# A hybrid decoder step on one core: natural keys in a tile of their own, late bias stores on a second semaphore, the first norm on five columns, and two conv units that share one wait

## What is computed

```python
n = rms_norm(x, g_mix);  q, k, v, hc, bc, cc = split(n @ w_in)
q, k = rms_norm(q, q_norm), rms_norm(k, k_norm)          # per head
attn = dilated_attention(q, k, v, rel_bias)              # dilations 1, 4, 16; the bias depends on the distance
conv = bc * short_conv(cc * hc, state_conv, conv_w)      # three taps
h = x + concat[rms_norm(attn, g_attn_out), rms_norm(conv, g_conv_out)] @ w_out
h = h + (silu(rms_norm(h, g_ffn) @ w_gate) * (rms_norm(h, g_ffn) @ w_up)) @ w_down
y = h + sigmoid(rms_norm(h, g_ple) @ w_ple_gate) * (p @ w_ple_proj)
```

## Time and profile before

| what | value |
|---|---|
| median of 3 runs | 2585.83 us (2585.45 to 2592.28) |
| profiled execution | 2585.61 us, of it span 2584.1 us, so 1.5 us around it |
| mean granted PE clock | 0.989 |
| PE busy | 2516.5 us (97%) |
| DVE, ACT, POOL busy | 1751.8 (68%), 950.2 (37%), 286.9 us (11%) |

### The profile page before, as it was taken

One profiled execution on the slowest core, in us unless ns is written; L12 is line 12 of the kernel. 1 busy time (PEld: TensorE's weight loads), 2 busy tenths in 40 slices (PEclk: granted clock), 3 DMA queues, 4 the chain that ended last, 5 costly groups with the idle time before them and its releaser, 6 DMA issues.

```text
span 2584.1 us, 52528 instructions
## 1 busy us (share of the span) xinstructions
PE 2516.5 (97%) x20677; PEld 2497.8 (97%) x20677; DVE 1751.8 (68%) x2181; ACT 950.2 (37%) x1283; POOL 286.9 (11%) x335
## 2 busy tenths in 40 slices
PE   8898999999989989999999999999999999999998
PEld 7898999999989979999999999999999999999998
DVE  3566777777686879889888898888433322466332
ACT  5333333343342444444444444444322211233221
POOL 2111111111021000000000000000000000142101
PEclk9999999999999989999999999999999999999999
DMA  6544333434344344445444454444665543233331
GB/s 194 159 114 126 107 112 103 122 106 113 99 127 132 118 115 115 134 130 145 130 114 133 129 144 130 114 134 130 209 207 173 159 141 116 80 89 101 107 109 58
DMA packets 482496, 328.31 MB, mean 127 GB/s; under 512 B 19382, under 2 KB 458714, under 8 KB 481400
## 3 DMA queue, kind: packets, MB, share of 16 engines
q1 hardware_dynamic: 451936, 250.74, 34.6%
q0 software_dynamic: 28848, 75.06, 9.0%
q10 hardware_dynamic: 1648, 1.65, 0.2%
HBM read 286.80 MB, written 44.91 MB: 128 GB/s over the span
## 4 chain that ended last, share of the span: by engine, by line
PE 88%; DMA 4%; DVE 4%; ACT 2%; issue 2%; POOL 0%; SPq 0%; ACTq 0%; DVEq 0%; POOLq 0%
PE acc L552 16%; PE acc L556 16%; PE acc L554 16%; PE acc L779 11%; PE acc L778 11%; PE acc L780 11%; DMA wraw<-in_w_in 2%; DMA wraw<-in_w_down 1%; ACT whi L924 1%; PE aux L594 1%; DVE wlo L1297 1%; PE aux L562 1%; DMA x_nat<-in_x_prompt 1%; PE aux L638 1%; PE aux L567 0%
## 5 line engine op out<-in xcount | busy, mean ns | idle before, releaser
L1297 DVE TENSOR_TENSOR wlo<-wraw,whi 128x1024 fp32r<-128x1024 f32 (+1 forms) x276 | 332.5, 1205 | 424.9 <-ACT whi L924 424.2
L924 ACT ACTIVATE whi<-wraw 128x1024 fp32r<-128x1024 f32 (+1 forms) x276 | 285.2, 1034 | 704.9 <-PE acc L556 593.4
L778 PE MATMUL acc<-xb_hi,whi 128*128 128x260 f32 x1232 | 349.2, 283 | 12.4 <-DVE xb_lo L1655 12.4
L779 PE MATMUL acc<-xb_lo,whi 128*128 128x260 f32 x1232 | 349.5, 284 | 0.0
L780 PE MATMUL acc<-xb_hi,wlo 128*128 128x260 f32 x1232 | 348.9, 283 | 0.0
L780 PE MATMUL acc<-xa_hi,wlo 128*128 128x260 f32 x1232 | 348.7, 283 | 0.0
L779 PE MATMUL acc<-xa_lo,whi 128*128 128x260 f32 x1232 | 348.5, 283 | 0.0
L778 PE MATMUL acc<-xa_hi,whi 128*128 128x260 f32 x1232 | 348.4, 283 | 0.0
L552 PE MATMUL acc<-slots_a,whi 128*128 128x260 f32 x1536 | 315.0, 287 | 0.0
L556 PE MATMUL acc<-slots_a,wlo 128*128 128x260 f32 x1536 | 310.2, 283 | 0.0
L554 PE MATMUL acc<-slots_a,whi 128*128 128x260 f32 x1536 | 308.4, 282 | 0.0
(11 more groups left out here) (308 smaller groups left out, 5099.7 us busy)
## 6 DMA issues: line engine op xcount, KB each, us to landing
wraw<-in_w_in SPq DMA_DIRECT2D x96, 512.0 KB, 4.0
blocks<-in_w_gate SPq DMA_DIRECT2D x88, 512.0 KB, 6.3
blocks<-in_w_up SPq DMA_DIRECT2D x88, 512.0 KB, 6.2
wraw<-in_w_down SPq DMA_DIRECT2D x48, 448.0 KB, 3.8
wraw<-in_w_out SPq DMA_DIRECT2D x32, 512.0 KB, 3.9
wraw<-in_w_ple_gate SPq DMA_DIRECT2D x32, 512.0 KB, 4.0
slots_b<-f_dram SPq DMA_DIRECT2D x28, 520.0 KB, 4.8
f_dram<-sig_t POOLq DMA_DIRECT2D x22, 520.0 KB, 3.3
```

The source lines that it names most:

```text
L778: mm(to, w_h, hi[:, n, X_OF[u], :], start=p == 0, stop=False)
L779: mm(to, w_h, lo[:, n, X_OF[u], :], start=False, stop=False)
L924: on(whi[:, u % HILO, 0:width], wraw[:, u % RAW, 0:width], ACT.Copy).then_inc(s_whi, 1)
L1297: V.tensor_tensor(wlo[:, u % HILO, 0:width], wraw[:, u % RAW, 0:width], whi[:, u % HILO, 0:width].bitcast(F32), ALU.subtract).then_inc(s_w ...
```

## The change

It has four parts. **Keys:** the natural keys get a place of their own, row 15 of `hid` (row 1 of `prob` in the last pair); their copy waits for the transposes alone, the next copy of values for the split of the values instead. In the last pair DVE's work is put in another order. **Bias stores:** S4 to S7 count on a semaphore of their own, the `load_skew` behind S7 waits for S0 to S3 alone, POOL waits for the others ahead of its loop, and S1 to S3 go out after units 8, 9 and 10. **First norm:** ACT takes the roots of the five columns ahead of its loop, DVE their reciprocals, PE then spreads the results, and DVE copies them out. **Conv half:** the first two units do seven tiles each, then the eighth; the norm's sum yields five columns, which are rooted, inverted and spread like the first; the attention of the last pair starts one unit later.

```diff
-    k_nat = v_nat
+    k_nat, k_nat_last = hid[:, KT - 1, 0:SEQ], prob[:, 1, :]
# ACT, heads, g == 9 (values) and g == 11 (keys)
+                    act.wait_ge(s_v2, j)
                 on(v_nat[:, :, :], ..., ACT.Copy).then_inc(s_natsb, 1)
...
-                    act.wait_ge(d_k, 16 * j)
-                act.wait_ge(d_v, 16 * j + 16)
-                act.wait_ge(s_v2, j + 1)
-                on(k_nat[:, :, :], ..., ACT.Copy).then_inc(s_natsb, 1)
+                on(k_nat_last if last else k_nat, aux[:, BANK_T, :], ACT.Copy).then_inc(s_natsb, 1)
# POOL
-                pool.wait_ge(d_skew, 16 * KA)
+                pool.wait_ge(d_skew, 16 * 4)
             load_skew(a + 1)
...
-            pool.wait_ge(s_unit, 6 + 2 * n)
+            pool.wait_ge(s_unit, 7 + n)
             store_skew(2 * n, 2 * n + 2)
# first norm: PE, ACT, DVE
-                    pe.wait_ge(s_xsq, QB + 1)
+                    pe.wait_ge(s_ninv, N_X)
                     for b in range(QB):
                         nc.tensor.transpose(aux[:, BANK_S, ...], gsq[:, b:b + 1].broadcast_to([P, P]), ident[:, :])
...
+        on(gsq[:, 0:QB], gsq[:, 0:QB], ACT.Sqrt, bias=EPS, scale=1.0 / D_MODEL)
+        on(gsq[0:DEC, QB:QB + 1], ..., ACT.Sqrt, ...).then_inc(s_nroot, 1)
         pair(FIRST, 0, None)
...
+            if a is None and g == 3:
+                dve.wait_ge(s_nroot, N_X)
+                V.reciprocal(gsq[:, 0:QB], gsq[:, 0:QB])
+                V.reciprocal(gsq[0:DEC, QB:QB + 1], ...).then_inc(s_ninv, 1)
+            if a is None and g == 4:
+                dve.wait_ge(s_nsum, N_X)
+                V.tensor_copy(rstd[:, 0:SEQ], aux[:, BANK_S, :])
+                V.tensor_copy(rstd[:, SEQ:T], aux[:, BANK_D, 0:DEC]).then_inc(s_xwide, 1)
-                V.reciprocal(rstd[:, :], rstd[:, :]).then_inc(s_ninv, 1)
# conv half, PE
-            if i == 0:
-                mm(aux[:, BANK_D, 0:HALF], ones[:, :], acc_conv[:, 0:HALF], ...)
-                mm(aux[:, BANK_O, 0:HALF], ones[:, :], acc_conv[:, HALF:T], ...).then_inc(s_nsum, 1)
+        for i in range(2):
+            unit(at, i, mixed, range(KC - 1), i, True, False, (s_x, KT + 1) if i == 0 else None, signal=False)
+        unit(at, 0, mixed, (KC - 1,), 0, False, True, (s_x, KT + KC), n0=KC - 1)
+        for b in range(QB):
+            mm(aux[:, BANK_D, b:b + 1], acc_conv[:, b * P:(b + 1) * P], ones[:, 0:1], start=True, stop=True)
+        unit(at, 1, mixed, (KC - 1,), 1, False, True, n0=KC - 1)
+        pe.wait_ge(s_ninv, N_CONV)
+        for b in range(QB):
+            nc.tensor.transpose(aux[:, BANK_O, ...], gsq[:, b:b + 1].broadcast_to([P, P]), ident[:, :])
# last pair and conv half, DVE
-        conv_lo(KC - 1)
-        norm_q(KA - 1, KA - 2)
-        q_lo(KA - 1)
...
-                V.reciprocal(rstd[:, :], rstd[:, :]).then_inc(s_ninv, 1)
+                V.reciprocal(gsq[:, 0:QB], gsq[:, 0:QB])
...
+            if i == 1:
+                q_lo(KA - 1)
```

More of the change, by code:

```diff
@@ L535, in _, with unit @@
         mm = nc.tensor.matmul
-        def unit(at, u, operand, tiles, slot, first, last, ready=None, between=None):
+        def unit(at, u, operand, tiles, slot, first, last, ready=None, between=None, n0=0, signal=True):
             pe.wait_ge(s_wlo, at.count(u))
@@ L677, in pair @@
                 n = g // 2
-                if a is None and g == 1:
+                if a is None and g == 2:
                     small_inputs()
@@ L1061, in square_x @@
             on(x_trash, x_nat[:, b, :], ACT.Square, accum_out=gsq[:, b:b + 1]).then_inc(s_xsq, 1)
-        square_x(0)
-        square_x(1)
+        for b in range(3):
+            square_x(b)
         act.wait_ge(s_tr0, KT + 3)
@@ L1070, in _ @@
            ).then_inc(s_cp0, 1)
-        for b in range(2, QB):
-            square_x(b)
+        square_x(3)
         act.wait_ge(s_xsq, QB)
         on(x_trash[0:DEC, :], xs_nat[:, :], ACT.Square, accum_out=gsq[0:DEC, QB:QB + 1]).then_inc(s_xsq, 1)
+        act.wait_ge(s_xsq, QB + 1)
+        on(gsq[:, 0:QB], gsq[:, 0:QB], ACT.Sqrt, bias=EPS, scale=1.0 / D_MODEL)
+        on(gsq[0:DEC, QB:QB + 1], gsq[0:DEC, QB:QB + 1], ACT.Sqrt, bias=EPS, scale=1.0 / D_MODEL).then_inc(s_nroot, 1)
         pair(FIRST, 0, None)
@@ L1085, in _ @@
         conv_hi(KC - 1)
-        q_hi(KA - 1)
         for i in range(KT):
@@ L1473, in heads @@
                 done.then_inc(s_qk2, 1)
[L1474 to L1480, removed]
-                    dve.wait_ge(s_pad, 1)
-                dve.wait_ge(s_u, j + 1)
-                V.tensor_scalar(conv[:, :], u_t[:, 2:2 + T], tap(2), None, ALU.mult).then_inc(s_tap, 1)
-                for n, t in enumerate((1, 0)):
-                    dve.wait_ge(s_tap, 5 * j + (2 * n + 1))
-                    V.scalar_tensor_tensor(conv[:, 0:SEQ], u_t[:, t:t + SEQ], tap(t), conv[:, 0:SEQ],
-                                           ALU.mult, ALU.add).then_inc(s_tap, 1)
-                    V.scalar_tensor_tensor(conv[:, SEQ:T], old[:, :, t], tap(t), conv[:, SEQ:T],
-                                           ALU.mult, ALU.add).then_inc(s_tap, 1)
+            if g == 10 and not last:
+                conv_taps(j, a)
                 v_lo(j)
-                if not last:
-                    q_lo(j)
+                q_lo(j)
             if g == 11:
@@ L1495, in heads @@
                 scaled(gate_t[:, :], 1, rstd).then_inc(s_read, 1)
+                if last:
+                    v_lo(j)
+                    conv_taps(j, a)
                 dve.wait_ge(s_read, 6 * j + 6)
@@ L1512, in pair @@
             for g in range(PAIR_UNITS):
-                split(at, g + HILO)
+                if not (last and g == PAIR_UNITS - 1):
+                    split(at, g + HILO)
                 if a is not None:
@@ L1519, in pair @@
                         conv_lo(c)
+            if last:
+                conv_lo(KC - 1)
+                split(at, PAIR_UNITS - 1 + HILO)
+                norm_q(KA - 1, KA - 2)
         def conv_lo(c):
@@ L1905, in attention, with store_rows @@
             add_squares(acc_attn, hid[:, a, :], 4 * a + (SQ_X + 2))
-        def store_rows(j):
+        def store_rows(j, last=False):
+            keys = k_nat_last if last else k_nat
             at = bass.ts(j, P)
@@ L1955, in store_skew @@
                               ap=[[BIAS_W, last - first], [-1, P], [1, SEQ]])
-            pool.dma_start(skew_dram[first:last], shifted).then_inc(d_skew, 16)
+            pool.dma_start(skew_dram[first:last], shifted).then_inc(d_skew if first < KA else d_skew2, 16)
         store_skew(0, 2)
@@ L1983, in _, with pair @@
         add_squares(acc_conv, hid[:, KA, :], SQ_X)
-        def pair(a, fresh=False):
+        def pair(a, fresh=False, last=False):
             attention(a, fresh)
-            store_rows(a + 1)
+            store_rows(a + 1, last)
             pool.wait_ge(s_conv, a + 2)
@@ L1991, in _ @@
         pair(0, fresh=True)
-        with pool.Fori(1, KA - 1) as a:
+        pool.wait_ge(d_skew2, 64)
+        with pool.Fori(1, KA - 2) as a:
             pair(a)
+        pair(KA - 2, last=True)
         for i in range(KT):
```

104 lines of the change are left out of this document (66 added, 38 removed).

## The result

| | median | runs | ratio to before (95% interval) |
|---|---|---|---|
| before | 2585.45 us | 5 (2583.36 to 2592.28) | |
| changed | 2571.97 us | 5 (2569.65 to 2573.67) | 0.9947 (0.9932 to 0.9961) |
| forecast | 2573 us (2563 to 2583) | | |

The account below looks back on a forecast made before the run. PE was taken as the bound, busy 2516.5 of 2584.1 us, so only its waits and half clock count. A and B together 6.7, C 5.3 and D 0.8 sum to 12.8; 2585.6 less that gives 2573 us, range 2563 to 2583.

Parts of the forecast that it names:

- A: First pair: a new wait of about 9 us before the norm's spread, unit 8 ending at 92.3 against 88.46; costs 3.8.
- B: Start of the second pair: earlier stores and the keys' own place remove PE's wait; with A it gains 6.7.
- The rival of stores that land one after another: Slower case: S1 to S3 land in turn at 14.4 us each, second-pair loads behind S3; 2593 us, chance 0.06.
- C: Start of the third pair: the keys are copied at once, the bias load goes behind S7; gains 5.3, bounds 1.7 and 8.1.
- D: Conv half: third unit 3.1 us sooner, up to 2.3 paid at half clock; gains 0.8, bounds -1.5 and 4.

Follow-up runs that it names:

- the trace with the old norm: The changed kernel with its first norm as before (roots and reciprocals of 128x520, small inputs ahead of unit 1): 2571.12 us, 0.9948.
- the early reciprocals: The changed kernel with DVE's five-column reciprocals two splits sooner, ahead of its copy of v: 2574.43 us, 0.9958.
- the three spread stores: The changed kernel with early first norm, q scaled sooner, and S1 to S3 after units 10, 11, 12, against all three after unit 10 (2566.93 us): 2572.84 us.
- the three runs on it: The changed kernel with values and keys sharing a tile again, 2569.90 us; with the bias load behind all eight stores, 2570.74 us; with both, 2576.09 us.
- the last experiment: Conv half reordered (q's norm as in other pairs, two splits later, short roots and reciprocals ahead of splits) on the 2563.06 us kernel: 2560.11 us, 0.9901.

## Why the prediction was right, step by step

**A, the first norm.** The mechanism came as told: PE waited 9.51 us (about 9), and its transposes ended near 66.5 (66.4). By the working's own rows the wait would have been 7.6 (65.7 less 58.14); it is longer because PE came to it at 55.80, which costs nothing, since DVE ends it. Unit 8 ended at 90.8 rather than 92.3, because the half clock of 2.5 us that was taken over from another stretch was too dear: unit 5 started at 66.5, and its pairs of matmuls took 0.64 us until 68.9 and 0.40 from 69.2, so it met only some 2.5 us of the low clock and lost half of that; the rest fell into the wait itself, where the clock was at 0.50 from 58.8 on. That A costs the whole kernel something is likely from the trace with the old norm (1.6 us at the second pair) and not shown by its time.

**B, the stores.** S1 to S3 left at 85.5, 91.2 and 97.9 (86, 92, 99) and S3 landed at 111.67 (113.3). That they count was shown: putting them back costs 7.0 us, and in the traces 6.4 between the first and the third transposes of the second pair (20.4 us against 14.0). The working had B at 10.5 (the 6.7 and the 3.8 that A costs), and 10.8 came (8.5 and 2.3). What the rest belongs to, no run of its own shows. The working named the keys' own tile with the stores. With the stores early it is worth nothing, but in the run with late stores it took the copy of the keys off a store that landed 13 us later, so here too two parts cut one chain; late stores and a shared tile together were not run. The rival of stores that land one after another is out: S1, S2 and S3 took 9.3, 10.2 and 13.8 us at distances of 6 us. What spoke against this part, that a load lands behind whatever store is under way, is what the experiments lived on: by it the late stores lost 7.0 us, the early reciprocals their gain, and the three spread stores a good part of their 5.9. The Trainium skill's rule on strongly ordered increments (DMA: Bandwidth & Descriptors, Queues, rings and completion order) fits the rows of the late stores (4.9 us ahead of the store, 13.1 beside it, landing 2.9 after it). That it is this order and not shared bandwidth, no run here tells, and the order alone does not cover all: with the spread stores one load took 10.1 us, though it landed 5.7 behind S2 and 4.6 ahead of S3.

**C, the third pair.** It gained 12.4 - 8.5 = 3.9, forecast 5.3. Three terms of the sum were off. The bias load ahead of the weight load cost 1.9 (16.9 less 15.0) where 1.5 was taken, inside the bound of 3.9. And PE still waited 3.84, so that it worked for 3.35 us at half clock and lost 1.7 of the 2.5 that the earlier trace rows had; 1.2 had been given to the gain, 0.8 came. From the late split to the transposes it took 7.54 (204.91 to 212.45), where the working had 7.10 (1.06, 5.24 and 0.8, the last from no row). Some 0.2 stays open. Where the working was wrong is the cause: it gave the gain to the copy of the keys, which no longer waits. Either that or the early bias load is enough, as the three runs on it show; the two parts are the same cure twice, and the second brings a cost with it: without it PE's second transposes came 3.4 us sooner in the trace.

**D, the conv half.** The third unit started at 730.63; less the 12.4 us that it was ahead already, that is 2.3 us sooner (3.1), and after the half clock 0.5 was left (0.8). PE waited 4.03 and 1.59 with transposes between, near the 6 us of the working. The gain is given back at the lower clock, as forecast; that DVE's norm of q and a split, which stand ahead of the short reciprocals, make the wait of 4.03, the last experiment shows by moving both: 0.25 was left.

The median of 2571.97 lies 1 us from the forecast in part by luck, since these errors had opposite signs: A and B together were 1.8 too low, C 1.4 and D 0.3 too high.

## What to carry to other kernels

A large transfer that nobody waits for still has to be given a place: here spreading three stores over two more units, so that the last left 11 and 14 us later, cost 6 to 7 us in two different kernels, because the loads that PE needed next went out beside them and took 10 to 13 us. In an engine's ordered list, ask of each short instruction which long wait stands just ahead of it; two reciprocals of 0.3 us together held PE for 9.5. Then ask what comes next: taking that wait away by itself gained nothing. Where two edits cut the same chain, undo them one at a time and then both, or each will look worthless or each will be given the whole gain.

## What the runs showed of the hardware that was not expected

A store of 512 KB from DRAM to DRAM in rows of reversed order took 9 to 18 us in the kernels before and after, a weight load of the same size 3.9 at the median of the changed kernel and up to 16.9 beside one. Not every transfer was held: with the late stores three of 1 and 4 KB went out between 116.4 and 117.5 and landed in 3.6 to 4.0 us, while S3 was under way until 126.86; a fourth of 4 KB took 11.6. Three stores of 512 KB sent within 2.2 us (at 92.77, 93.87 and 94.94) landed at 98.16, 100.19 and 111.21 (5.4, 6.3 and 16.3 us each), so 18.4 us for all three, where three sent 6 us apart took 26 from the first start to the last landing (85.47 to 111.67). And the low clock can fall into the wait before it costs work: in the wait of 9.51 us (55.8 to 65.3) it stood at 0.50 by 58.8, and PE then worked for 3.6 us at 1.2 GHz (65.3 to 68.9). Behind a wait of 3.84 us PE worked for 3.4 us at that level, and behind one of 2.11 for none.
